# Splitting each weight piece of the mixing phases in two halves, a chunk apart

## What is computed

```python
h = rmsnorm(x, norm_mix[l])
mkv = rmsnorm(mem, norm_mem) @ w_mem_kv[l]              # 256 memory tokens
q, k, v, qm = split(h @ w_in[l])                        # 12 heads of 64, 4 memory heads
y_tok = windowed_gqa(q, k, v, sink) if l == 0 else neighbourhood_attn(q, k, v, rpb)
y_mem = memory_attn(qm, mk, mv)
x = x + concatenate([y_tok, y_mem]) @ w_out[l]
h = rmsnorm(x, norm_ffn[l]); gate, up = split(h @ w_gate_up[l])
x = x + (silu(gate) * up) @ w_down[l]
```

## Time and profile before

| what | value |
|---|---|
| median of 3 runs | 1061.81 us (1060.62 to 1061.88) |
| the profiled execution | 1061.81 us, of which the span is 1059.9 us |
| busy TensorE / VectorE / ScalarE / GpSimd | 1011.5 / 729.0 / 562.3 / 119.7 us |
| granted TensorE clock, mean | 0.991 |
| mixing phase of layer 0 / layer 1 | about 23 to 134 us / 323 to 440 us |

### The profile page before, as it was taken

One profiled execution on the slowest core, in us unless ns is written; L12 is line 12 of the kernel. 1 busy time (PEld: TensorE's weight loads), 2 busy tenths in 40 slices (PEclk: granted clock), 3 DMA queues, 4 the chain that ended last, 5 costly groups with the idle time before them and its releaser, 6 DMA issues.

```text
span 1059.9 us, 14098 instructions
## 1 busy us (share of the span) xinstructions
PE 1011.5 (95%) x5524; PEld 857.3 (81%) x5524; DVE 729.0 (69%) x980; ACT 562.3 (53%) x796; POOL 119.7 (11%) x179
## 2 busy tenths in 40 slices
PE   6898999999999989999999999999989999999996
PEld 4676887889888877888888877888767789999885
DVE  5768764566356568578888667688866667877753
ACT  6557664444345558643443445596556456555541
POOL 0123140000000013200000010122540000000001
PEclk9999999999999999999999999999999989999998
DMA  9765579655555531389999796546545436555541
GB/s 346 285 168 81 158 203 294 194 187 179 178 200 188 168 120 42 119 304 351 344 334 334 283 358 204 198 136 212 195 160 179 159 114 224 167 193 179 161 138 40
DMA packets 107377, 214.02 MB, mean 202 GB/s; under 512 B 4400, under 2 KB 32320, under 8 KB 103920
## 3 DMA queue, kind: packets, MB, share of 16 engines
q1 hardware_dynamic: 102640, 196.39, 54.3%
q0 software_dynamic: 4384, 16.51, 6.6%
q10 hardware_dynamic: 288, 0.23, 0.1%
HBM read 208.39 MB, written 6.15 MB: 202 GB/s over the span
## 4 chain that ended last, share of the span: by engine, by line
PE 74%; DVE 10%; ACT 6%; DMA 4%; issue 4%; POOL 1%; DVEq 0%; SPq 0%; ACTq 0%; POOLq 0%
PE bank L916 19%; PE bank L918 19%; PE bank L917 19%; PE bank L933 4%; PE bank L935 4%; PE bank L934 4%; DVE lo L1680 4%; ACT hi L1238 3%; PE bank L892 3%; DMA raw<-in_w_gate_up 2%; PE bank L945 1%; DMA raw<-in_w_in_a 1%; PE bank L894 1%; PE bank L1083 1%; DMA early<-in_memT 1%
## 5 line engine op out<-in xcount | busy, mean ns | idle before, releaser
L1680 DVE TENSOR_TENSOR lo<-raw,hi 128x2048 fp32r<-128x2048 f32 (+2 forms) x164 | 364.8, 2228 | 213.2 <-ACT hi L1238 212.9
L1238 ACT ACTIVATE hi<-raw 128x2048 fp32r<-128x2048 f32 (+2 forms) x164 | 303.4, 1855 | 247.8 <-PE bank L918 141.3
L916 PE MATMUL bank<-hi,xTh 128*128 128x512 f32 (+2 forms) x688 | 267.5, 389 | 2.4 <-DVE lo L1680 2.4
L918 PE MATMUL bank<-hi,xTl 128*128 128x512 f32 (+2 forms) x688 | 261.1, 380 | 0.0
L917 PE MATMUL bank<-lo,xTh 128*128 128x512 f32 (+2 forms) x688 | 260.8, 379 | 0.0
L916 PEld LDWEIGHTS bank<-hi,xTh 128*128 128x128 f32 x688 | 130.1, 189 | 27.3 <-DVE lo L1680 3.2
L918 PEld LDWEIGHTS bank<-hi,xTl 128*128 128x128 f32 x688 | 129.8, 189 | 25.0
L917 PEld LDWEIGHTS bank<-lo,xTh 128*128 128x128 f32 x688 | 130.1, 189 | 22.4
L916 PE MATMUL bank<-hi,hTh 128*128 128x512 f32 x264 | 103.3, 391 | 0.2 <-DVE lo L1680 0.2
L918 PE MATMUL bank<-hi,hTl 128*128 128x512 f32 x264 | 102.8, 389 | 0.0
L917 PE MATMUL bank<-lo,hTh 128*128 128x512 f32 x264 | 102.8, 389 | 0.0
(11 more groups left out here) (361 smaller groups left out, 1417.6 us busy)
## 6 DMA issues: line engine op xcount, KB each, us to landing
raw<-in_w_gate_up SPq DMA_DIRECT2D x44, 1024.0 KB, 6.9
raw<-in_w_down SPq DMA_DIRECT2D x30, 1024.0 KB, 5.1
raw<-in_w_ada SPq DMA_DIRECT2D x24, 1024.0 KB, 7.0
raw<-in_w_up SPq DMA_DIRECT2D x22, 1024.0 KB, 5.1
raw<-in_w_in SPq DMA_DIRECT2D x20, 1024.0 KB, 5.1
raw<-in_w_out SPq DMA_DIRECT2D x12, 1024.0 KB, 5.0
raw<-in_w_in_b SPq DMA_DIRECT2D x10, 1024.0 KB, 5.1
raw<-in_w_in_a SPq DMA_DIRECT2D x6, 1024.0 KB, 11.8
```

Source lines behind the costliest of these rows:

```text
L916: e.matmul(o, sh, h[:, k, :], start=p.first and k == 0, stop=False)
L918: done = e.matmul(o, sl, h[:, k, :], start=False, stop=p.last and k == p.nk - 1)
L1238: e.activation(hi_s[m % SPLITS][:, 0:n], raw[p.at % RAWS][:, 0:n], ACT.Copy).then_inc(hi_made, 1)
L1680: e.tensor_tensor(lo_s[s][:, 0:n], raw[p.at % RAWS][:, 0:n], hi_s[s][:, 0:n].bitcast(F), ALU.subtract).then_inc(lo_made, 1)
```

## The change

The split of a piece becomes two steps, each of one half of the piece's columns on both engines. Outside the mixing phases both are done as before (a piece in one: `("split", m, 0, 2)`). While `halving` is on, from the start of `mix` up to its last `drain()`, the first half stands where the split stood, after chunk 0 of part m, and the second half is put after chunk 1 of part m, behind the tasks of `between()` and ahead of the tile's evacuation. The semaphore counts follow: `lo_ready(m)` is the count after the piece's last half, for TensorE and for the loads alike.

```diff
 def split_through(self, m):
     ...
-                self.steps.append(("split", m))
+                if self.halving:
+                    self.steps.append(("split", m, 0, 1))
+                    self.second_halves.append(("split", m, 1, 2))
+                else:
+                    self.steps.append(("split", m, 0, 2))
             self.split_next += 1
+
+    def finish_splits(self):
+        self.steps.extend(self.second_halves)
+        self.second_halves = []
 ...
 def part(...)
             self.steps.append(("mm", m, ch))
             if ch == 0 and not self.hold:
+                self.finish_splits()
                 self.split_through(self.owed)
+            elif ch == 1:
+                self.finish_splits()
             if ch < p.chunks - 1:
                 between()
 ...
 def mix(self, l):
+        self.halving = True
 ...
+        self.halving = False
         self.drain()
 ...
 def lo_ready(m):
-            return lo_made, m + 1
+            return lo_made, order.split_at[m]
 ...
 # ScalarE
-                    m, n = p.m, p.nk * p.w
+                    m, n = p.m, p.nk * p.w // 2
+                    cut = slice(n * name[1], n * name[2])
-                    e.activation(hi_s[m % SPLITS][:, 0:n], raw[p.at % RAWS][:, 0:n], ACT.Copy).then_inc(hi_made, 1)
+                    e.activation(hi_s[m % SPLITS][:, cut], raw[p.at % RAWS][:, cut], ACT.Copy).then_inc(hi_made, 1)
 ...
 # VectorE
-                    n, s = p.nk * p.w, p.m % SPLITS
-                    e.wait_ge(hi_made, p.m + 1)
-                    e.tensor_tensor(lo_s[s][:, 0:n], raw[p.at % RAWS][:, 0:n], hi_s[s][:, 0:n].bitcast(F), ALU.subtract).then_inc(lo_made, 1)
+                    n, s = p.nk * p.w // 2, p.m % SPLITS
+                    cut = slice(n * name[1], n * name[2])
+                    e.wait_ge(hi_made, order.split_by[step])
+                    e.tensor_tensor(lo_s[s][:, cut], raw[p.at % RAWS][:, cut], hi_s[s][:, cut].bitcast(F), ALU.subtract).then_inc(lo_made, 1)
```

More of the change, by code:

```diff
@@ L153, in __init__ @@
         self.summed_by = {}
+        self.halving, self.second_halves = False, []
         self.res_at = {}
@@ L556, in count @@
         self.high_at, self.exp_at, self.begun_at = {}, {}, {}
-        high = exp = begun = 0
+        high = exp = begun = splits = 0
+        self.split_at, self.split_by = {}, {}
         for step in self.steps:
             kind = step[0]
-            if kind in ("memx", "xin"):
+            if kind == "split":
+                splits += 1
+                self.split_by[step] = self.split_at[step[1]] = splits
+            elif kind in ("memx", "xin"):
                 high += 2
```

## The result

The changed kernel takes 1068.02 us (median of 6 runs, 1066.62 to 1070.07), the kernel before beside it 1061.85 us (6 runs, 1060.62 to 1063.3): a ratio of 1.0053, 95% interval 1.0039 to 1.0068. It is slower by some 6 us, where 1065.2 was forecast, and lies above the range. The profiled execution took 1068.08 us, its span is 1066.1.

The account below looks back on a forecast made before the run. TensorE, busy 95% of the span, was taken as the bound, so only its waits count. Terms of -0.1 + 0.5 + 0.93 and 0.6 + 0.5 + 0.93 gave +3.4 us: 1065.2 us, range 1062.3 to 1067.0.

Parts of the forecast that it names:

- start: Start of the first mixing phase, splits 6 to 8: later transposes, but scores(0) loses its wait; -0.1 us, or +0.4.
- split 14: First layer's attention: the second half delays soften(14) and soften(15), which GpSimd's normalising of head 14 awaits; +0.5 us.
- split 17: First layer's handover to the feed-forward: the second half runs ahead of the residual sum; +0.93 us.
- splits 56, 57: Second layer, two pieces close together: the query tile's staging comes late, making its transposes wait; +0.6 us.
- split 62: Second layer's attention, near 417 us: the same delay as at split 14 in the first; +0.5 us.
- split 65: End of the second layer's mixing: the residual sum is late as at split 17; +0.93 us.
- Right: Signs: waits near 111.3 and 417.9 no shorter, residual waits near 1.9, scores(0) unwaited, new wait near 364, soften(13) sooner, soften(14) later.
- The step that failed: Claimed clock 1.00 in the stretch holding most of the first layer's attention and the DMA-bound one behind it.
- The swallowing: Late weights behind the first layer's mixing absorb that layer's +1.3 us, giving 1063.8 us; chance 0.22.
- the fixed costs: All 26 halved pieces' extra instruction costs, 0.09 + 0.10 us each, fall on the path: +4.9, 1066.7 us; chance 0.08.
- a load late by a whole landing: A piece for split 15 or 16 lands 5.0 us late and stalls TensorE, giving 1070 us; chance 0.05.
- The faster rival: In attention the second half is not held behind the exp, so waits go: -2.5 us, 1059.3 us; chance 0.10.

Follow-up runs that it names:

- experiment 9: The changed kernel with TensorE multiplying ready operands ahead of four waits of 1.5 us and more, nothing moved; 1066.71 us, ratio 1.003 to the kernel before.
- experiment 8: The changed kernel run once more, unaltered, for a second profile and times; 1068.54 us, ratio 1.0039 to the kernel before.
- experiment 6: Exactly the change's 26 pieces halved, the second half right behind the first, against the kernel before; 1060.19 us, ratio 0.9964.
- experiment 3: Only pieces 17 and 65, the last of each mixing phase, halved a chunk apart, against the kernel before; 1066.15 us, ratio 1.0022.
- experiment 4: The kernel before, no halves, with three small VectorE maxima ahead of each mixing phase's last residual sum, written to a new buffer; 1070.69 us, ratio 1.0064.
- experiment 5: The kernel before, no halves, with three small VectorE maxima ahead of each mixing phase's last residual sum, written to an old buffer's free columns; 1066.57 us, ratio 1.0026.
- experiment 10: Only pieces 14, 56, 57 and 62 halved a chunk apart, against the kernel before; 1066.4 us, ratio 1.0026.
- experiment 11: The changed kernel with pieces 17 and 65 whole, the other 24 halved a chunk apart; 1067.21 us, ratio 1.0043 to the kernel before.
- experiment 2: Only the 19 pieces the prediction priced at nothing halved a chunk apart, against the kernel before; 1060.81 us, ratio 0.9977.
- experiment 7: Every weight piece halved, the second half right behind the first, against the kernel before; 1054.19 us, ratio 0.9892.

## Why the prediction failed, by its own steps

This table sets TensorE's transposes or scores against the same ones of the kernel before (start minus start, us). The left column is the time in the kernel before; "filled" is experiment 9, "again" experiment 8.

| before | what | predicted sum | changed | again | filled |
|---|---|---|---|---|---|
| 83.59 | start | -0.1 | +1.32 | -0.16 | -0.15 |
| 110.86 | split 14 | +0.4 | +1.83 | +0.32 | +0.40 |
| 133.43 | split 17 | +1.33 | +2.79 | +1.31 | +1.38 |
| 158.89 | feed-forward | +1.33 | +4.39 | +2.94 | +1.38 |
| 183.76 | DMA-bound stretch | +1.33 | +2.26 | +3.37 | +2.03 |
| 363.32 | splits 56, 57 | +1.93 | +2.99 | +4.14 | +2.94 |
| 395.01 | scores of layer 1 | +1.93 | +3.84 | +4.97 | +2.94 |
| 417.42 | split 62 | +2.4 | +4.20 | +5.32 | +3.44 |
| 439.43 | split 65 | +3.4 | +5.24 | +6.36 | +4.44 |
| 499.92 | feed-forward of layer 1 | +3.4 | +6.84 | +6.36 | +4.42 |
| 556.95 | second DMA-bound stretch | +3.4 | +6.64 | +6.50 | +5.41 |
| 633.12 | third block | +3.4 | +6.91 | +6.53 | +5.61 |
| span | | +3.4 | +6.2 | +6.7 | +4.7 |

**The waits were right.** Read from the filled kernel, where the clock plays no part, the terms are -0.15 (forecast -0.1), +0.55 (+0.5), +0.98 (+0.93), +0.91 (+0.6), +0.50 (+0.5) and +1.00 (+0.93): 3.8 against 3.4. The one that is off is splits 56 and 57. Every sign that the prediction lists under "Right" came, and the time still left the range. The tasks moved as forecast. After split 14 in the changed kernel (VectorE):

```profile
104.13 0.48 DVE L1521 CUSTOM_DVE_ANT_0 early<-bank,const,small 128x256 f32<-128x256 f32 x1
...
108.27 0.48 DVE L1521 CUSTOM_DVE_ANT_0 early<-bank,const,small 128x256 f32<-128x256 f32 x1
...
110.63 0.48 DVE L1521 CUSTOM_DVE_ANT_0 early<-bank,const,small 128x256 f32<-128x256 f32 x1
```

These are soften(13), (14) and (15), at 104.70, 106.18 and 108.81 before. With the 1.32 us by which all was late here, they moved by -1.89, +0.77 and +0.50 us; forecast were -1.9, +0.75 and +0.5.

**The start, and the root.** The pair's transposes were forecast at 41.07 and stood at 40.97; scores(0) lost its wait. GpSimd's root ended at 38.50 (forecast 38.6):

```profile
36.88 1.62 POOL L1922 TENSOR_TENSOR rms<-rms,small 128x2 f32<-128x2 f32 x1 [4.72 <-DVE rms L1459]
```

It starts inside a half-size low part (36.70 for 1.22 us on VectorE) and ends 0.58 us behind that part's end; before, it took 2.68 us beside a whole one, and the root before it 0.71. (The prediction says that the root was done 0.7 us after the low part's end; its rows give 35.40 + 2.68 - 35.22 - 2.29 = 0.57, the same as now.) That agrees with the lock of the shared ports which the prediction drew from the Trainium skill, "SBUF — State Buffer", section "SBUF: two separate sides".

**The step that failed** is the sentence "The granted clock is full (1.00) in both stretches". It is true of the kernel before, and the sum carried it over to the changed one, whose waits are longer: the start's from 1.51 to 2.60 us, the handovers' from 0.96 and 0.80 to 1.91 and 1.90. The waiting time itself was priced, what TensorE does behind it was put at nothing. At the lower clock three matmuls of 128x512 take 1.28 us (starts at 138.10 and 139.38) where they take 0.68. The price is read from the table: +1.5 from the start's wait (+1.32 against -0.16 at 83.59), +1.6 from the first handover's (2.79 to 4.39; +1.63 in the run again), +1.6 from the second handover's (5.24 to 6.84, where the run again and the filled one stay as they were), and +0.85 behind the wait of 1.56 us at 391.72. That last wait was not new: from those transposes to the scores it is 6.28 us before (388.73 to 395.01), 7.13 in the changed kernel, 6.29 in the filled one. It stands unfilled in twelve profiles, and the clock fell behind it in three, both of the changed kernel and that of experiment 6, which has none of the longer waits; so it is not shown that this 0.85 us comes from the change.

That the waits make the clock fall is what experiment 9 shows, as far as one profile and five runs go: work put into them, and nothing else, brings back 1.00 in all four stretches and the mean clock of the kernel before. That each of them does it each time is refuted by experiments 3, 4, 5 and 8. Counted over the thirteen profiles, in the first two layers (20 to 470 us), the lower clock came with 9 of the 15 waits of TensorE of 1.8 us or more, with 3 of the 20 between 1.5 and 1.8 us, and with none of the 37 between 1.4 and 1.5. The Trainium skill, "TensorE: Matmul & The Clock Gate", section "HAM oscillation — how this bites in real kernels", says that gaps in TensorE's work bring it back to the lower clock; the traces agree in kind, with gaps of 1.56 to 2.71 us here, shorter than that section's, of which only some were followed by it.

What the clock costs on the mean is less than the first profile shows: with 0.984 that execution has the lowest mean clock of its six (0.984 to 0.989). In times: the changed kernel is at ratio 1.0053 or 1.0039, filled at 1.003, so the clock is worth 0.0009 to 0.0023 of 1062 us, 1.0 to 2.4 us; the mean clocks of experiment 8 gave some 2.4. The same estimate for experiments 3 and 5 (0.0005 and 0.0010 under the kernel before) is 0.5 and 1.0 us, which with their waits of 2.1 and 1.8 us gives 2.6 and 2.8, where 2.3 and 2.8 were measured. Without the clock the time is 1.003 x 1061.85 = 1065.0, next to the 1065.2 forecast. I would not lean on that agreement, for two more amounts happen to be small in sum:

**The swallowing** was a rival with chance 0.22, and it exists, but not reliably. In the changed kernel both waits of the earlier trace rows's second stretch (0.74 and 0.92 us in the kernel before) are gone, and the lag falls from 4.39 to 2.26. In the run again they are 1.12 and 1.00 and nothing is given back (2.94 to 3.37); in the filled kernel a wait of 2.44 us at 185.79 takes their place (1.38 to 2.03); in experiment 10 the lag falls from 0.58 to -0.33. The landing of those weights doesn't move with the work ahead of it in a fixed way.

**The second DMA-bound stretch**, 500 to 560 us, was in no step. From 439 to 633 us the lag grows by 1.67, 0.17 and 1.17 us in the three kernels of the table. In the first of them that is the clock (1.60 of it by 499.92, behind the second handover's wait); in the filled one it is late loads, as in experiments 10 and 11. Halves a chunk apart are not needed for it, since the wait near 557 also stands in experiments 4 and 5, without halves (0.67 and 1.30 us), and in 6, with the halves together (1.19); in the run again it is 0.14 and in the changed kernel's first profile nothing. The kernel before has one profile here, without that wait; how often it has it is not known. Whether the change makes these loads later on the mean stays open.

Of the other rivals, the fixed costs are refuted by experiments 2, 6 and 7, and a load late by a whole landing never showed. The faster rival was wrong for this order and right for another: with the second half next to the first (experiment 6) nothing is held behind the exp, the waits of 0.81 and 0.56 us fall to nothing and 0.35, and the kernel takes 1060.19 us on a chip where before takes 1063.69.

## What to carry to other kernels

A change that makes a wait of TensorE longer, where it is the busiest engine, costs the wait and may cost the clock behind it: look at the granted clock in and behind the waits of similar length elsewhere in the kernel (here 1.25 us at 633.12 and 3.81 at 770.46 in the third block, both with the lower clock), and keep its price as an end of the range. Splitting a piece in halves shortens what stands behind it when the halves stay together; set apart, the second one makes the next task late wherever TensorE waits for that task (19 pieces elsewhere, set apart, gained 2.4 us in experiment 2). A gain or a loss of 1 to 2 us ahead of a DMA-bound stretch can't be added to the end as it is: the stretch at 175 to 185 us took 2.1 us of it in one profile of the changed kernel and none in the other.

## What the runs showed of the hardware

**Moving buffers by 32 bytes a partition** cost about 4 us (ratios 1.0064 and 1.0026, each against the kernel before on its own chip). Experiments 4 and 5 differ only in where three small results go; in 4 a new buffer shifts all that is allocated behind it. TensorE's timeline of 4, then of 5:

```profile
590.17 0.40 PE L917 MATMUL bank<-hi,hTh 128*128 128x512 f32 x1
590.40 0.40 PE L918 MATMUL bank<-lo,hTh 128*128 128x512 f32 x1
...
593.67 0.40 PE L917 MATMUL bank<-hi,hTh 128*128 128x512 f32 x1
```

```profile
590.57 0.39 PE L916 MATMUL bank<-hi,hTh 128*128 128x512 f32 x1
590.79 0.39 PE L917 MATMUL bank<-lo,hTh 128*128 128x512 f32 x1
...
593.97 0.39 PE L916 MATMUL bank<-hi,hTh 128*128 128x512 f32 x1
```

From 590.17 to 593.67 are fifteen matmuls, 0.2333 us each; from 590.57 to 593.97 again fifteen, 0.2267 us each. The granted clock of 570 to 630 us is 1.00 in both. The spacing is 0.2333 in whole stretches of 4 (about 266 to 325, 570 to 635, 815 to 855 and 985 to 1055 us), and nowhere there in 5. The 4 us are rather a lower figure: the runs of 4 had the higher mean clock (0.989 to 0.993, against 0.985 to 0.991 in 5). What about the address does it wasn't tried.

**Halves in place** gain in the third block too. In the kernel before the low part begins 1.93 us behind the high one for a whole piece and 1.07 for a half; with every piece halved the wait of 3.81 us at 770.46 is 3.23 and that of 1.33 at 790.18 is 0.55, and the page has 1011.3 us of TensorE work against 1011.5. 164 instructions more on each of VectorE and ScalarE (1144 and 960) cost them 14.9 and 15.5 us of busy time, and TensorE's did not grow.
